# The last two down steps of each feed-forward half, done token tile by token tile

## What is computed

```
h = rms_norm(x, norm_g[i, 2*s]) * (1 + scale) + shift
g, u = split(h @ w1)              # w1: 1024 x 5632, so g and u are 256 x 2816
y = (silu(g) * u) @ w2            # w2: 2816 x 1024
x = x + 0.5 * gate * rms_norm(y, norm_g[i, 2*s + 1])
```

## Time and profile before

| | |
|---|---|
| median of the three executions | 3866.25 us (3865.9, 3866.25, 3875.92) |
| span of the profiled execution | 3875.5 us |
| its own time | not given apart; the one execution that fits the span took 3875.92 us, 0.4 us more |
| PE busy | 3151.6 us, 81% of the span |
| VectorE (DVE) busy | 2452.2 us, 63% |
| ScalarE (ACT) busy | 1294.1 us, 33% |
| PE's granted clock, mean | 0.868 of full speed |
| the first feed-forward half's last down matmul | starts at 1642.91 us |
| the last half's last down matmul | starts at 3867.37 us |

### The profile page before, as it was taken

One profiled execution on the slowest core, in us unless ns is written; L12 is line 12 of the kernel. 1 busy time (PEld: TensorE's weight loads), 2 busy tenths in 40 slices (PEclk: granted clock), 3 DMA queues, 4 the chain that ended last, 5 costly groups with the idle time before them and its releaser, 6 DMA issues. The chain is left out here.

```text
span 3875.5 us, 53219 instructions
## 1 busy us (share of the span) xinstructions
PE 3151.6 (81%) x21732; PEld 2669.1 (69%) x21732; DVE 2452.2 (63%) x3818; ACT 1294.1 (33%) x2068; POOL 569.5 (15%) x310
## 2 busy tenths in 40 slices
PE   3965776566665659988999998899998899997899
PEld 3854665322221129987898996898997799987798
DVE  3654553788888867736586854686853686543654
ACT  1003321111111123436434345434344434342733
POOL 0001001344444520030000013000004000012000
PEclk9966787777766679987999997999998999996999
DMA  4971001899999968631585842484943484553143
GB/s 184 403 304 44 2 3 57 307 368 375 382 369 390 391 285 353 228 145 44 218 323 209 355 146 97 194 340 190 367 155 124 190 344 152 185 184 121 45 175 129
DMA packets 118255, 860.09 MB, mean 222 GB/s; under 512 B 15152, under 2 KB 16304, under 8 KB 17712
## 3 DMA queue, kind: packets, MB, share of 16 engines
q1 hardware_dynamic: 80912, 588.77, 39.4%
q0 software_dynamic: 36864, 268.45, 17.3%
q10 hardware_dynamic: 288, 0.26, 0.0%
HBM read 856.38 MB, written 1.05 MB: 221 GB/s over the span
## 5 line engine op out<-in xcount | busy, mean ns | idle before, releaser
L252 PE MATMUL ps<-h_hi,w_hi 128*128 128x256 f32 x3328 | 951.7, 286 | 38.4 <-DVE h_lo L533 16.0
L254 PE MATMUL ps<-h_hi,w_lo 128*128 128x256 f32 x3328 | 947.4, 285 | 0.0
L253 PE MATMUL ps<-h_lo,w_hi 128*128 128x256 f32 x3328 | 947.4, 285 | 0.0
L179 DVE TENSOR_TENSOR w_lo<-w_ring,w_hi 128x2048 fp32r<-128x2048 f32 x284 | 649.7, 2290 | 466.4 <-ACT w_hi L174 464.8
L174 ACT ACTIVATE w_hi<-w_ring 128x2048 fp32r<-128x2048 f32 x330 | 630.0, 1914 | 683.1 <-PE ps L254 556.6
L252 PEld LDWEIGHTS ps<-h_hi,w_hi 128*128 128x128 f32 x3328 | 640.7, 193 | 52.1 <-issue 22.0
L253 PEld LDWEIGHTS ps<-h_lo,w_hi 128*128 128x128 f32 x3328 | 640.5, 192 | 3.2
L254 PEld LDWEIGHTS ps<-h_hi,w_lo 128*128 128x128 f32 x3328 | 640.5, 192 | 0.0
L2958 PE MATMUL ps<-expert_rows,expert_diag 128*128 128x512 f32 x512 | 381.0, 889 | 290.3 <-ACT expert_diag L2996 290.1
L179 POOL TENSOR_TENSOR w_lo<-w_ring,w_hi 128x2048 fp32r<-128x2048 f32 x46 | 212.2, 4632 | 2276.4 <-ACT w_hi L174 2276.4
L2958 PEld LDWEIGHTS ps<-expert_rows,expert_diag 128*128 128x128 f32 x512 | 120.7, 259 | 544.6 <-ACT expert_diag L2996 442.6
(11 more groups left out here) (454 smaller groups left out, 4319.7 us busy)
## 6 DMA issues: line engine op xcount, KB each, us to landing
w_ring<-in_w_stream SPq DMA_DIRECT2D x360, 1024.0 KB, 4.9
a_ring<-in_a_stream SPq DMA_DIRECT2D x128, 1152.0 KB, 11.0
a_ring<-in_m_stream SPq DMA_DIRECT2D x24, 1024.0 KB, 9.7
mod_acc<-in_mod_start SPq DMA_DIRECT2D x6, 2304.0 KB, 8.8
alibi<-in_alibi SPq DMA_DIRECT2D x3, 2048.0 KB, 8.7
expert_rows<-in_experts,expert_idx POOLq DMA_INDIRECT x256, 9.2
a_ring<-in_norm_post_row SPq DMA_DIRECT2D x3, 1024.0 KB, 4.7
na_bias<-in_na_bias SPq DMA_DIRECT2D x1, 2048.0 KB, 8.0
```

The costliest lines, as they stand in the source:

```text
L179: pool.tensor_tensor(self.w_halves(n)[1], self.w_item(n), self.w_halves(n)[0], ALU.subtract).then_inc(self.lo_made, 1)
L252: pe.matmul(out, stationary[0], moving[0], start=start, stop=False)
L253: pe.matmul(out, stationary[0], moving[1], start=False, stop=False)
L254: return pe.matmul(out, stationary[1], moving[0], start=False, stop=stop)
```

## The change

PE's program alone changes. The body of `down` that fills one bank becomes a function, `down_half`. The loop runs three turns in place of four, and its last turn is written out: up(9), down(8), up(10). The last two steps are then done together by `down_two`: first all waits of both steps, then for token tile 0 the 12 matmuls of down(9) and the 12 of down(10), then the same for token tile 1. `y_ready` is signalled as before, once for each bank after its last matmul. `w_used` for item 31 is signalled after down(9)'s share of token tile 1, which is the 36th of the 48 matmuls; before, it was signalled after the 24th. The number of matmuls stays the same.

```
             def down(s, i=0):
                 pe.wait_ge(hidden.sem, i * 2 + hidden.at(s + 1))
                 core.split_wait(pe, down_item(s), i)
-                (its own loop over t, half and m)
-                        if s == FF_STEPS - 1:
-                            last.then_inc(tail.y_ready.sem, 1)
-                if s < FF_STEPS - 1:
-                    last.then_inc(w_used, 1)
+                for t in range(TT):
+                    for half in range(2):
+                        last = down_half(s, t, half)
+                last.then_inc(w_used, 1)
+
+            def down_two(s):
+
+                pe.wait_ge(hidden.sem, hidden.at(s + 2))
+                core.split_wait(pe, down_item(s))
+                core.split_wait(pe, down_item(s + 1))
+                for t in range(TT):
+                    for half in range(2):
+                        last = down_half(s, t, half)
+                    if t == TT - 1:
+                        last.then_inc(w_used, 1)
+                    for half in range(2):
+                        down_half(s + 1, t, half).then_inc(tail.y_ready.sem, 1)
...
-            with pe.Fori(0, FF_TURNS, 1) as i:
+            with pe.Fori(0, FF_TURNS - 1, 1) as i:
                 up(3, i)
                 down(2, i)
                 up(4, i)
                 down(3, i)
-            down(FF_STEPS - 1)
+            up(FF_STEPS - 2)
+            down(FF_STEPS - 3)
+            up(FF_STEPS - 1)
+            down_two(FF_STEPS - 2)
```

More of the change, by code:

```diff
@@ L723, in up, with down_half @@
                     last.then_inc(w_used, 1)
+            def down_half(s, t, half):
+                halves = [w.rearrange("p (m k) n -> p m (k n)", m=2) for w in core.w_halves(down_item(s))]
+                for m in range(2):
+                    last = in_three(pe, core.y[:, 2 * t + half, :],
+                                    [h[:, s % 2, m, t * P:(t + 1) * P] for h in hid],
+                                    [w[:, m, half * BANK:(half + 1) * BANK] for w in halves],
+                                    s == 0 and m == 0, s == FF_STEPS - 1 and m == 1)
+                return last
             def down(s, i=0):
@@ L727, in down @@
                 core.split_wait(pe, down_item(s), i)
-                halves = [w.rearrange("p (m k) n -> p m (k n)", m=2) for w in core.w_halves(down_item(s))]
                 for t in range(TT):
                     for half in range(2):
[L731 to L735, removed]
-                        if s == FF_STEPS - 1:
-                            last.then_inc(tail.y_ready.sem, 1)
-                if s < FF_STEPS - 1:
-                    last.then_inc(w_used, 1)
+                        last = down_half(s, t, half)
[11 more added lines that the diff above has]
+                        down_half(s + 1, t, half).then_inc(tail.y_ready.sem, 1)
             up(1)
```

## The result

| | |
|---|---|
| changed kernel, four executions | median 3933.65 us (3929.34 to 3935.44) |
| kernel before beside it, four executions | median 3871.09 us (3865.9 to 3883.9) |
| ratio | 1.0153, 95% interval 1.0133 to 1.0173 |
| ratio in a second comparison (last experiment) | 1.0164, 1.0140 to 1.0188 |
| spans of the profiled executions | 3930.3 us after, 3875.5 us before: +54.8 |

The change makes the kernel 1.5% slower. 1.0153 of 3866.25 is 3925.4, inside the forecast range of 3896 to 3932; the median of the four executions is 1.7 us above its top.

The account below looks back on a forecast made before the run. PE bounds the inside of a half, a ScalarE and VectorE chain hanging on item 31's release the tail. Waits and releases 37.0, tail clock 13.7 and wait clock 2 sum to 52.7, say 53 us: 3866.25 + 53 = 3919, range 3896 to 3932.

Parts of the forecast that it names:

- The written-out code at 0: PE's last loop turn written out as straight code: no matmul more, no stall, cost 0.
- The wait of 2.18 us, nothing covers it: PE idles before down_two's first matmul for the last hidden values: 2.18 us in seven halves, 2.53 in the seventh half.
- The rival in which the release hides and only waits are paid: Something other than item 34 holds the tail, so only the waits cost: 17.6 us, 3884; chance 0.08.
- The release of item 31, 2.74 us later plus the wait: ScalarE's split of item 34 and the squares behind it start later: 4.92 us in six halves, 5.3 in the seventh.
- The last half, gain 0.02 from the tile order: Last half, without item 34: earlier tile 0 gains 0.02 us, the wait of 2.18 stays, so +2.2.
- The later loads at 0: SP's queue: load of item 37 starts 4.92 us later, that of item 38 2.18 us later, cost 0.
- The clock in the tail, 13.7: Six modulation halves: small matmuls start later, so more pass at the low clock, 13.7 us, bounds 0 and 16.
- "fewer than ten" small matmuls at the full clock: Profile sign in the tail: small matmuls start 3.4 us after the last down matmul, fewer than ten at full clock.
- The clock at the new wait, one in six: After down_two's wait the clock falls in one in six of eight waits: about 2 us, bounds 0 and 12.
- The rival with the clock falling at most of the new waits: Clock falls after most of down_two's waits too: 37 + 13.7 + 12 = 63 us, 3929; chance 0.12.
- the faster one: Rival: squares start when their bank is complete, tile 1's final addition 2.3 us earlier in seven halves: 3850; chance 0.04.
- no change: Rival: PE's order or waits cover the wait after all and the gain is eaten: 3866; chance 0.04.

Follow-up runs that it names:

- last experiment: The changed kernel as it is, timed once more against the kernel before, beside the changed kernel with the wait filled by 9 unread matmuls: 1.0164.
- the release alone: Item 31 released late without the early wait, against the kernel before: 1.0082 with the new tile order, 1.0068 with the old.
- the moved split: Item 34 split after the tail's squares, against the kernel before: 1.0037 in the changed kernel, 0.9968 also without its early wait, 0.9971 in the kernel before.
- the fill: Changed kernel plus 14 unread 512-column matmuls between the last down matmul and the small matmuls of six modulation halves: 1.0114 against the kernel before.
- the wait alone: Kernel before with its order kept, but the wait for the last step's hidden values placed ahead of down(9): 1.0054 against the kernel before.

## Why the prediction was right, point by point

**The written-out code at 0**: right, 0.9999.

**The wait of 2.18 us, nothing covers it**: right to about 0.01 us in each of the eight halves. The rival in which the release hides and only waits are paid is out, since the release alone costs 0.7 to 0.8%.

**The release of item 31, 2.74 us later plus the wait**: right. The first square came 14.15 us after the last up matmul, 5.05 later than before; the forecast had 4.92, and 0.1 is the slower start after the wait. (Where the clock fell at the wait it came 1.6 us later still.) That ScalarE's queue holds the squares back is shown by the moved split: with it the squares follow their banks.

**The last half, gain 0.02 from the tile order**: too small to be seen. With the late wait its stretch is 19.01 us, before 19.01. The cost of 2.2 from the wait came.

**The later loads at 0**: nothing speaks against it; outside the eight stretches the changed kernel has no more than the scatter between profiles.

**The clock in the tail, 13.7**: measured 13.1 (12.5 in the second profile), and the fill shows that PE's idleness ahead of the small matmuls costs this, since the full clock runs out while nothing is done with it. That it came so close is in part luck: with the wait alone the same six tails were 4.0 us longer with no later start of the small matmuls. And the sign of "fewer than ten" small matmuls at the full clock came in five of six halves; the third had 13.

**The clock at the new wait, one in six**: the step that was mis-sized. I took the share from the six waits of the earlier trace rows, of which one was followed by the low clock, and put 2 us for eight waits; it was four of eight, 6.4 us. Over the five profiles that have this wait unfilled it is 16 of 40. The six waits were the right kind of case, but one profile of them was too few, and it happened to be the mildest. Waits of 2.0 to 2.7 us for `w_lo` near the start of a half are in all twelve profiles, and 31 of 57 were followed by the low clock (48 matmuls of 256 columns took 7.0 to 7.2 us in place of 5.7); the profile of before, with its one of six, has the smallest share of all. Taking 0.4 gives 8 x 0.4 x 1.6 = 5 us and a forecast of 3922. The rival with the clock falling at most of the new waits was about as near as the forecast: the stretches grew by 57.4, between 52.7 and 63.

**The slower start after a wait**, 0.11 us in each half, 0.9 in all, wasn't in the sum.

**The rivals**: neither the faster one nor no change came. The experiments show how the faster one would have had to look: wait and release taken away, and then it is the moved split that gains. Its 2.3 us earlier addition of tile 1 did come with the moved split (12.9 us after the first down matmul, before 1647.43 - 1632.15 = 15.3), in either tile order, but the seven halves shortened by only 1.3 to 1.4 us on average: in the six modulation halves the transposes start 0.1 to 0.2 us after the last small matmul, when their first input has been there for 0.7 to 5.4 us.

## What to carry to other kernels

Before reordering work so that a result is there sooner, look at what the consumer's queue has in front of the consumer: here ScalarE stood at a split that waited for a ring slot, and the reordering held that slot longer. When a step is moved ahead of others, the step that it passes may have been the cover of somebody's latency; price the wait that becomes bare. Moving one prefetch behind the urgent work gained 0.3% where the reordering lost 1.5%. And take the share of waits after which the clock falls from several profiles: one profile had one in six, all twelve together 31 of 57.

## What the runs showed of the hardware

An idle time of only 2.0 to 2.4 us on PE, between dense stretches of more than 10 us, was followed by the clock of 1.2 GHz in 16 of 40 cases, for about 1.6 us of loss each time; filled with matmuls that nothing reads, it was followed by it in none of eight. The Trainium skill, "TensorE: Matmul & The Clock Gate", section "HAM oscillation — how this bites in real kernels", describes this fall for waits for DMA, of some 3 to 5 us, between bursts of matmuls, at each of them. These runs agree that it happens, after shorter waits too, though not at every one. Small matmuls with two columns, issued without a gap at 0.112 us, don't keep the full clock: it fell 2.0 to 5.2 us after the last dense matmul over the runs, while PE did the small ones or was still idle ahead of them, a wider spread than the 3.3 to 4.6 of the kernel before. And 48 down matmuls behind a wait took 0.11 us longer where the clock stayed, in 22 of 24 cases (0.3 in the other two), and as much in the eight cases in which the wait was filled.
